# Normed head values by DMA crossbar instead of TensorE transposes, and r projected two heads later

## The reference, cut to what matters

```python
u = rms_norm(h, g_pre); proj = u @ w_in          # split: c_b c_c c_x c_z | q k v r lr_f lr_b | m_a m_b
y_conv = c_b * conv3(c_c * c_x) * silu(c_z);      p_conv = y_conv @ w_out_c
o = gla(q, k, v, g_f) + reversed_gla(q, k, v, g_b)   # 4 heads, 128 keys, 256 values each
o = rms_norm(o, gla_g)                            # per head and token, over its 256 values
y_gla = o * silu(r);                              p_gla = y_gla @ w_out_g
merged = sigmoid(m_a) * p_conv + sigmoid(m_b) * p_gla
out = h + rms_norm(merged @ w_out, g_post)
```

## Time and profile before

| | us |
|---|---|
| median of 3 runs (lowest, highest) | 2988.17 (2987.7, 2990.24) |
| profiled execution, its own time | 2986.59 |
| span of its slowest core, core 1 | 2985.0 |
| spans of the eight cores | 2977.7 to 2985.0 |
| granted TensorE clock, mean of each core | 0.995 to 0.997 |

### The profile page before, as it was taken

How to read it: one execution, slowest core, us unless ns; L and a number is a source line. 1 busy time by engine, 2 the same in 40 slices (tenths; PEclk the granted TensorE clock), 3 DMA queues, 4 the chain that set the end, 5 groups by cost and what they waited for, 6 DMA issues and landing times.

```text
span 2985.0 us, 54382 instructions; the slowest of 8 cores (2977.7 to 2985.0 us)
## 1 busy us (share of the span) xinstructions
PE 2923.8 (98%) x16828; PEld 1521.0 (51%) x16828; DVE 1575.0 (53%) x2467; ACT 1337.3 (45%) x2546; POOL 833.5 (28%) x1260
## 2 busy tenths in 40 slices
PE   6899999999999999999999999999999999999998
PEld 3465554444456655444455555444445655544443
DVE  4576771452567775153267677326227776723523
ACT  5666641231476663132167665223236666412211
POOL 3133243321322332142232223223122222311212
PEclk9899999999999999999999999999999999999999
DMA  7456557842632233273372223347245222323323
GB/s 183 80 101 132 98 146 156 233 135 78 172 92 63 54 85 98 75 231 105 92 188 61 55 63 80 103 126 210 78 128 145 57 64 57 107 75 106 118 77 124
DMA packets 258071, 330.56 MB, mean 111 GB/s; under 512 B 136432, under 2 KB 139376, under 8 KB 257280
## 3 DMA queue, kind: packets, MB, share of 16 engines
q1 hardware_dynamic: 244256, 301.73, 35.1%
q0 software_dynamic: 13536, 25.37, 5.9%
HBM read 265.80 MB, written 59.31 MB: 109 GB/s over the span
## 4 chain that ended last, share of the span: by engine, by line
PE 95%; DMA 1%; DVE 1%; issue 1%; ACT 1%; POOL 0%; SPq 0%; DVEq 0%; ACTq 0%; POOLq 0%
PE ps L477 94%; PE ps L482 1%; DMA sb_KT<-sb_GR 0%; DMA sb_onT<-x 0%; DVE sb_TF L507 0%; DMA sb_SM<-sb_GR 0%; ACT sb_GR L494 0%; ACT L494 0%; DMA sb_ycT<-x 0%; SPq L534 0%; DMA y<-sb_ycT 0%; DVE sb_ycT L503 0%; DVE sb_ycT L507 0%; POOL sb_stat L512 0%; ACT sb_AT L494 0%
## 5 line engine op out<-in xcount | busy, mean ns | idle before, releaser
L477 PE MATMUL ps<-sb_uT,sb_W 128*128 128x512 bf16 (+2 forms) x8960 | 1875.4, 367 | 4.0 <-ACT sb_onT L494 3.7
L477 PEld LDWEIGHTS ps<-sb_uT,sb_W 128*128 128x128 bf16 (+1 forms) x8960 | 818.7, 98 | 932.2 <-issue 19.5
L494 ACT ACTIVATE sb_CS<-ps 128x512 f32<-128x512 f32 (+2 forms) x640 | 348.6, 550 | 935.7 <-PE ps L477 933.5
L507 DVE SCALAR_TENSOR_TENSOR sb_CS<-sb_CS,ps 128x512 f32<-128x512 f32 x256 | 176.1, 688 | 686.2 <-PE ps L477 680.7
L503 POOL TENSOR_TENSOR sb_GR<-sb_CS 128x512 bf16<-128x512 f32 x128 | 162.2, 1268 | 692.9 <-DVE sb_CS L507 692.8
L477 PE MATMUL ps<-sb_GR 128*128 128x512 bf16 (+2 forms) x1792 | 348.7, 318 | 0.0
L507 DVE SCALAR_TENSOR_TENSOR sb_CS<-sb_CS,sb_convw 128x512 f32<-128x512 bf16 x256 | 215.1, 850 | 73.3 <-ACT sb_CS L494 58.6
L477 PE MATMUL ps<-sb_V,sb_uT 128*128 128x256 bf16 x2048 | 241.5, 273 | 0.0
L477 PEld LDWEIGHTS ps<-sb_GR 128*128 128x128 bf16 x1792 | 163.8, 98 | 135.6 <-issue 0.7
L477 PE MATMUL ps<-sb_onT,sb_W 128*128 128x512 bf16 x1024 | 231.5, 379 | 0.0
L503 POOL TENSOR_TENSOR sb_CS<-sb_CS 128x512 f32<-128x512 f32 x128 | 166.0, 1301 | 178.1 <-DVE sb_CS L507 160.8
(11 more groups left out here) (116 smaller groups left out, 2653.3 us busy)
## 6 DMA issues: line engine op xcount, KB each, us to landing
sb_W<-wsc SPq DMA_DIRECT2D x496, 256.0 KB, 2.8
sb_onT<-x SPq DMA_DIRECT2D x50, 512.0 KB, 5.7
sb_W<-w_all POOLq DMA_DIRECT2D x80, 256.0 KB, 5.3
sb_GR<-x SPq DMA_DIRECT2D x40, 512.0 KB, 5.3
wsc<-sb_W SPq DMA_DIRECT2D x80, 256.0 KB, 4.5
y<-sb_GR SPq DMA_DIRECT2D x32, 512.0 KB, 3.2
sb_ycT<-x SPq DMA_DIRECT2D x32, 512.0 KB, 5.1
y<-sb_ycT SPq DMA_DIRECT2D x32, 512.0 KB, 3.8
```

What stands on the lines that cost most here:

```text
L477: S.add("pe", lambda e: e.matmul(out, lhsT=lhsT, rhs=rhs, start=start, stop=stop), r, w, cost=max(0.025, free_n(rhs) / 2400.0 + 0.0025) / ...
L494: S.add("act", lambda e: e.activation(out=out, in_=in_, func=func, **kw), r, w, table=TABLE.get(func), cost=0.17 + 0.82e-3 * free_n(in_) + ...
L507: S.add("dve", lambda e: e.scalar_tensor_tensor(out=out, in0=in0, scalar=scalar, in1=in1, op0=op0, op1=op1), r, w, cost=0.21 + 1.05e-3 * f ...
```

## The change

The four TensorE transposes of a unit and their PSUM bank go away. A DMA transpose (`b_X`, on SP) takes the 128x512 values of ON straight to onT, which is now laid out by tile: for a head 16 tiles of 2 x 128 columns. ON has three buffers instead of two, and `b_O` of unit u asks for the transfer of unit u - 3 where it asked for the transposes of u - 2. r of head s - 2 is projected in step s, so r of head 2 in the last step of phase 1; that of head 3 follows behind it, and half of it stands inside `stage6`, ahead of the first og. Its Silu stays in its PSUM bank, which is held until `r_mul` on DVE multiplies it with `glag` and with onT, in place. og reads onT with a stride. The scan of `soft` is cut in two halves of 512, the loads of the next x into onT are contiguous, and the planner counts 3.5 us for a DMA transpose and has other values of `PWEIGHT` and `BACKLOG`.

```diff
+XBAR_LAT = 3.5
-PRESS, PWEIGHT = 4.0, 0.5
-BACKLOG = 4.0
+PRESS, PWEIGHT = 4.0, 1.0
+BACKLOG = 3.0
...
-        for c in ("M", "BO", "BS", "BT", "BM", "BN", "EM", ...
+        for c in ("M", "BO", "BS", "BX", "RM", "BM", "BN", "EM", ...
...
-        onT = [Buf("onT", j * 4096, 4096) for j in range(8)]
+        onT = [Buf("onT", h * 8192, 8192) for h in range(4)]
-        ON = [Buf("ON", i * KB, KB) for i in range(2)]
+        ON = [Buf("ON", i * KB, KB) for i in range(3)]
...
-            S.add("dve", lambda e: e.tensor_tensor_scan(out=r_ap, data0=smask[:], data1=r_ap, initial=0.0,
-                                                        op0=ALU.mult, op1=ALU.add), e_k + ["smask"], e_k, cost=2.3)
+            for z in range(2):
+                h_ap, h_k = e1(F32, d * 1024 + z * 512, 512)
+                r_ap = h_ap[:, ::-1] if d else h_ap
+                S.add("dve", lambda e, r_ap=r_ap: e.tensor_tensor_scan(out=r_ap, data0=smask[:], data1=r_ap, initial=0.0,
+                                                                       op0=ALU.mult, op1=ALU.add), h_k + ["smask"], h_k, cost=1.22)
...
-        def b_T2(H, u):
-            n0 = 6 - 2 * (u % 4)
-            tb, tbk = npsb()
-            for dvh in range(2):
-                for z in range(2):
-                    s_ap, s_k = ON[u % 2](BF16, z * 256 + dvh * 128, 128)
-                    c = dvh * 256 + (1 - z) * 128
-                    tr(tb[:, c:c + 128], s_ap, s_k, tbk)
-            for dvh in range(2):
-                o_ap, o_k = onT[H.hd * 2 + dvh](BF16, H.t0 + n0 * 128, 256)
-                stt(o_ap, tb[:, dvh * 256:(dvh + 1) * 256], glag[:, dvh:dvh + 1], o_ap, ALU.mult, ALU.mult,
-                    tbk + o_k + ["glag"], o_k)
+        def b_X(H, u):
+            n0 = 6 - 2 * (u % 4)
+            s_ap, s_k = ON[(H.hd * 8 + u) % 3](BF16)
+            o_ap, o_k = onT[H.hd](BF16, (H.half * 8 + n0) * 256, 512)
+            dtr(o_ap.rearrange("p (c k) -> p c k", c=4), s_ap, s_k, o_k, ("ox", (H.hd * 8 + u) % 3), 1 << 17)
+
+        def onv(j, t, n):
+            ap, keys = onT[j // 2](BF16, t * 256, n * 256)
+            keys = [k for i in range(n) for k in onT[j // 2](BF16, (t + i) * 256 + (j % 2) * 128, 128)[1]]
+            return ap.rearrange("p (i d k) -> p i d k", i=n, d=2)[:, :, j % 2, :], keys
...
-            bank, bk = nps()
+            bank, bk = nps(True)
             proj(h, 0, 128, s * 512, 512, bank, bk)
-            o_ap, o_k = onT[j](BF16, s * 512, 512)
-            act(o_ap, bank[:, 0:512], AF.Silu, bk, o_k)
-            if s == 3:
-                rel(h)
+            act(bank[:, 0:512], bank[:, 0:512], AF.Silu, bk, bk)
+            G["rb", j, s] = (bank, bk)
+
+        def r_mul(j, s):
+            bank, bk = G.pop(("rb", j, s))
+            o_ap, o_k = onv(j, 4 * s, 4)
+            stt(o_ap, bank[:, 0:512].rearrange("p (i k) -> p i k", i=4), glag[:, j % 2:j % 2 + 1], o_ap, ALU.mult, ALU.mult,
+                bk + o_k + ["glag"], o_k)
+            drop(bk)
...
+        def r_items(b, h, j, qs):
...
+            for q in qs:
+                put("RM", lambda q=q: r_mul(j, q), ("rm", b, j, q),
+                    [("r", b, j, q), ("X", b, j // 2, 7 - 2 * q), ("X", b, j // 2, 6 - 2 * q)])
+            return [(lambda q=q: unit(q), ("r", b, j, q), [("X", b, j // 2, 7 - 2 * q), ("X", b, j // 2, 6 - 2 * q)]) for q in qs]
...
+                    rj = 2 * (s - 2) + half if s >= 2 else None
+                    ca, cz, cbb, rh = conv_units(b, s // 4, 2 * (s % 4) + half, rj)
+                    ru = [] if rj is None else r_items(b, rh, rj, range(4))
+                    for (fn, name, aft) in ca + ru[0:2] + cz + ru[2:4] + cbb:
+                        put("D2", fn, name, list(aft) + ([("ST", b, 7)] if s < 4 else []))
+                    if s == 4 and half == 1:
+                        rr = [(w2.reserve(("r", j)), j) for j in (6, 7)]
+                        last = [[it for (h, j) in rr for it in r_items(b, h, j, qs)] for qs in ((3, 2), (1, 0))]
...
-                            pu = (b, s - 1, u - 2) if u >= 2 else (b, s - 2, u + 6)
+                            pu = (b, s - 1, u - 3) if u >= 3 else (b, s - 2, u + 5)
...
-                            put("BT", lambda H=H, u=u: b_T2(H, u), ("T2", b, s - 1, u),
-                                [("M", b, s - 1, u), ("r", b, 2 * s - 1, 3)])
+                            put("BX", lambda H=H, u=u: b_X(H, u), ("X", b, s - 1, u), [("M", b, s - 1, u)])
...
-            osrc = lambda c, s: onT[c](BF16, t0 + s * 512, 512)
+            osrc = lambda c, s: onv(c, hh * 8 + 4 * s, 4)
...
+                if n == "og" and d == 0:
+                    for it in late:
+                        put("D2", *it)
```

More of the change, by code:

```diff
@@ L87, in __init__, with add @@
         self.starts = None
-    def add(self, eng, fn, reads=(), writes=(), semkey=None, extra=(), cost=0.1, table=None, nbytes=0):
+    def add(self, eng, fn, reads=(), writes=(), semkey=None, extra=(), cost=0.1, table=None, nbytes=0, lat=DMA_LAT):
         op = Op(eng, fn, semkey)
@@ L129, in add @@
             self.free["dma"] = d0 + nbytes / DMA_RATE
-            op.end = self.free["dma"] + DMA_LAT
+            op.end = self.free["dma"] + lat
         else:
@@ L536, in dtr @@
         def dtr(out, in_, r, w, semkey, nbytes):
-            return S.add("sp", lambda e: e.dma_start_transpose(out, in_), r, w, semkey=semkey, nbytes=nbytes)
+            return S.add("sp", lambda e: e.dma_start_transpose(out, in_), r, w, semkey=semkey, nbytes=nbytes, lat=XBAR_LAT)
         def rot(name, bufs):
@@ L633, in program @@
         yout = [[Buf(r, o + i * 4096, 4096) for i in range(2)] for r, o in (("GR", 40 * KB), ("ycT", 8 * KB))]
-        xst = onT + [Buf("GR", i * 4096, 4096) for i in range(8)]
+        xst = [Buf("onT", i * 4096, 4096) for i in range(8)] + [Buf("GR", i * 4096, 4096) for i in range(8)]
         usX = [Buf("ycX", i * 2048, 2048) for i in range(2)]
@@ L1034, in ycT, with conv_units @@
             return Buf("ycT", j * 2048, 2048)
-        def conv_units(b, hh, j, r=False):
+        def conv_units(b, hh, j, r=None):
             t0 = hh * 1024
             pv = pvb[j % 2]
-            hs = {n: w2.reserve((n, j)) for n in (("cc", "cx", "r", "z", "cb") if r else ("cc", "cx", "z", "cb"))}
+            hs = {n: w2.reserve((n, j if n != "r" else r)) for n in (("cc", "cx", "z", "cb") if r is None else ("cc", "cx", "r", "z", "cb"))}
             me = (b, hh, j)
@@ L1244, in phase1 @@
                                 [("v",) + me + (3,)] + ([("qm",) + me + (1,)] if pr == 3 else []))
[L1247 to L1255, removed]
+                    rj = 2 * (s - 2) + half if s >= 2 else None
[6 more added lines that the diff above has]
+                        last = [[it for (h, j) in rr for it in r_items(b, h, j, qs)] for qs in ((3, 2), (1, 0))]
+                        for it in last[0]:
+                            put("D2", *it)
+                        late = last[1]
                     if s > 0:
@@ L1312, in stage6 @@
             ysrc = lambda c, s: ycT(hh, c)(BF16, s * 512, 512)
-            osrc = lambda c, s: onT[c](BF16, t0 + s * 512, 512)
-            for d in range(8):
-                hs = [p.reserve((n, d)) for p, n in ((w1, "ma"), (w2, "oc"), (w1, "mb"), (w2, "og"))]
-                for s in range(2):
-                    put("D2", lambda h=hs[0], d=d, s=s: gate(h, d, s, "ta"))
-                for s in range(2):
-                    put("D2", lambda h=hs[1], d=d, s=s: outp(h, d, s, "t1", ysrc), ("oc", b, hh, d, s))
-                for s in range(2):
-                    put("D2", lambda h=hs[2], d=d, s=s: gate(h, d, s, "tb"), ("mb", b, hh, d, s))
-                for s in range(2):
-                    put("D2", lambda h=hs[3], d=d, s=s: outp(h, d, s, "t2", osrc), ("og", b, hh, d, s),
-                        [("T2", b, 3, 7)])
+            osrc = lambda c, s: onv(c, hh * 8 + 4 * s, 4)
+            hs = {}
+            seq = [(n, d) for d in range(8) for n in ("ma", "oc", "mb", "og")]
+            if late:
+                seq.remove(("ma", 1))
+                seq.insert(3, ("ma", 1))
+            for (n, d) in seq:
+                hs[n, d] = (w1 if n[0] == "m" else w2).reserve((n, d))
+            for (n, d) in seq:
+                if n == "og" and d == 0:
+                    for it in late:
+                        put("D2", *it)
+                for s in range(2):
+                    if n[0] == "m":
+                        put("D2", lambda h=hs[n, d], d=d, s=s, n=n: gate(h, d, s, "t" + n[1]), (n, b, hh, d, s))
+                    else:
+                        put("D2", lambda h=hs[n, d], d=d, s=s, n=n: outp(h, d, s, "t1" if n == "oc" else "t2", ysrc if n == "oc" else osrc),
+                            (n, b, hh, d, s), [("rm", b, 7, 0)] if n == "og" else [])
         def cast_wo(d):
@@ L1390, in program @@
         for z in range(4):
[L1391 to L1393 removed]
+            ap, keys = onT[z](F32, 0, 1024)
+            xnext.append((ap, keys))
```

(8 more changed lines are left out.)

57 lines of the change are left out of this document (26 added, 31 removed).

## The result

The changed kernel is faster: the ratio of its runs to those of the kernel before is 0.9885, 95% interval 0.9865 to 0.9904. Executions in which one die ran over 1% longer than the other at a lower granted clock, or which were over 1.5% above the fastest, are left out of every ratio here. The profiled execution took 2953.35 us, and its slowest core was core 7.

The account below looks back on a forecast made before the run. TensorE, busy 98% of the span, was taken as the bound; - 28.4 + 4 + 1.6 + 3 = - 19.8 from 2986.6 gave 2966.8, forecast as 2968 for the median run; own range 2959 to 2979, 8 in 10 2951 to 2982.

Parts of the forecast that it names:

- rival 1: Sequence 0's key waits go, nothing added: 2951; or transposes cost up to their busy time: 2947; chance 0.10 for both.
- Transposes, - 28.4: Removing 512 TensorE transposes saves their distance to the next start: 128 groups of four at 0.222 us, 28.4 us.
- Sequence 0, + 3: Sequence 0's start: heads 0 and 1 lose r as filler while weights still arrive, costing 3 us.
- Rival 2: Sequence 0 starves without r in its first heads, losing 27.7 us: 2987.5, no change; chance 0.09.
- Phase 1, + 4: Phase 1: the longer chain of squares, norm and transfer makes TensorE wait 1 us per sequence, 4 us in all.
- The first og, + 1.6: Ahead of each sequence's first og, TensorE waits for the last r product: 0.4 us each, 1.6 us in all.
- Edits at nothing: Transfers on SP's queue, strided og reads, Silu in PSUM and halved scans were each taken to cost TensorE 0 us.
- Busy time "down by about 50 us": Sign in the profile after: TensorE's busy time falls by about 50 us where the span falls by 20.
- Rival 3: SP's queue: key transposes come late behind transfers waiting for DVE, TensorE stops; just slower up to 3038; chance 0.07.
- Rival 4: Phase 1: DVE or ACT takes over as the bound; chance 0.02 together with the rest.

Follow-up runs that it names:

- Run 1: Changed kernel with 512 dead TensorE transposes of the identity put back, four ahead of each r unit: 2981.0 us, ratio 0.9976.
- run 4: Kernel before, with only r of head 0 in sequence 0 moved behind the conv units of both halves of step 0: 2981.3 us, ratio 0.9977.
- run 3: Changed kernel with the old planner constants (PWEIGHT 0.5, BACKLOG 4.0): 2972.1 us, ratio 0.9946.
- run 7: Changed kernel with r projected one head later instead of two, behind the conv units, none left inside `stage6`: 2975.1 us, ratio 0.9956.
- run 2: Kernel before with only the new planner constants (PWEIGHT 1.0, BACKLOG 3.0, 3.5 us for a DMA transpose): 2977.4 us, ratio 0.9964.
- run 5: Changed kernel with two ON buffers and each of the 128 transfers issued a second time into an unread scratch buffer: 2975.6 us, ratio 0.9958.

## Why the prediction was right, and where its sum was off

Faster was right, and so was the main term; the size was 20 where 34 was measured. 2953.8 lies below the forecast's own range (2959 to 2979) and within the range of 8 in 10 because that took in rival 1, which had a chance of 0.10: in that much it was luck. By its own steps:

- **Transposes, - 28.4.** Right. Run 1 gives 27, and each period is 7.0 us shorter against 28.4 / 4 = 7.1. The 81 ns a matmul of the Trainium skill ("TensorE: Matmul & The Clock Gate", "Back-to-back issue gap") gives, by the estimate in the prediction, 41.5 us; run 1 does not agree, with 53 ns.
- **Sequence 0, + 3: the step that failed.** The prediction said that "heads 0 and 1 no longer have r to fill TensorE". Measured is 12.9 like for like less the 7.1 of the transposes: - 5.8 instead of + 3, 9 us of the 14 by which the sum was off. In step 0, r was not filler. It waited for the last input tile and held the conv units behind it; runs 4, 3 and 7 fill the window 75 to 125 us whenever r stands behind, with either set of constants. The prediction had named what happened, that the new order avoids the two key waits and wins 8.9 us, and did not take it. The row was in the prediction ("the first 150 us are the one stretch where TensorE waits"), and the second rival put it down to the input's norm and the key transposes, without asking which item stood first in D2.
- **Phase 1, + 4.** Measured: the three periods lose 21.0 where the transposes alone give 21.3, so + 0.3 where three sequences had + 3. The fear had ground: with the old constants it is 5 us a sequence (run 3). The prediction gave `PWEIGHT` and `BACKLOG` no price at all; run 3 puts them at 18 us in the new arrangement and run 2, with the 3.5 us for a DMA transpose, at 11 in the old.
- **The first og, + 1.6.** Measured 0.7, four waits of 0.2.
- **Edits at nothing** (transfers, stride, Silu in PSUM, scans): right together, since the periods leave 0.3 us for all of them; none was run alone, so a loss of one could hide behind a gain of another. The strided og reads take 379 ns as before; the scan in two halves costs 147.7 us of DVE against 144.8, beside TensorE's work.
- **Busy time "down by about 50 us"**: wrong, it is 26.3. The busy time of the engine counts a moment once, so the tails, under which the next matmul runs, were never in the difference. The group's 49.6 and the engine's total are two kinds of sum.
- **Rival 1** (2951) lies within 3 us of the result, and half for its own reason: both key waits went, 8.9 us, and one of 4.8 came elsewhere. **Rival 2** was the wrong way round. **Rival 3** stayed away in the kernel: TensorE has no wait for a `sb_SM` or `sb_CS` transfer; the one stop of run 5, 10.7 us, came by POOL's queue. **Rival 4**: DVE has 228 of 340 us and ACT 195, less than before.

What stays open: how the 5.8 us of sequence 0 divide between the place of r and the constants. Each alone gains more than that in the old kernel (7 and 11 us), so they are not additive: early arrival is given back, in runs 2 and 4 behind the first og (3.8 and 9.3 us), in the changed kernel between 150 and 450 us (7.5 us of the 13.6 won in the window before). In the changed kernel under the old constants nothing of it is left at the og of sequence 1 (run 3).

## What to carry to other kernels

Where one engine is 98% busy, the price of taking instructions off it is their distance to the next start times their count, and putting them back as dead work measures it. Before an item is called filler, look at what it waits for and what stands behind it in its chain: in an in-order chain an item that comes too early is a plug. Ask the same of every in-order queue: in run 5 one weight load ahead of a small instruction on POOL had its part in a stop of 10.7 us on TensorE. When a change moves the order that a planner makes, price the planner's constants as a part of the change: here they decided 18 of 34 us.

## What the runs showed of the hardware

- The changed kernel moves 347 MB instead of 331, and in more packets: the page after counts 322,327 DMA packets against 258,071, and 206,064 under 512 B against 136,432. The median landing of the 128 transfers is 2.8 us. At the end of sequence 0, with the DMA engines over 90% busy in most slices, the same transfer took 7.0 us in run 5 (median of four), and 8.5 in the changed kernel (of two). The key transposes that TensorE waited for landed as slowly: 11.7 us for the one at 121 us before, 9.8 for the one at 287 us after, where the medians are 3.1 and 3.3.
- A stop of TensorE costs more than its length. Behind the 4.78 us wait of the changed kernel the next eight matmuls of 128x512 start 0.43 us apart, and those behind them 0.22:

```profile
287.15 0.58 PE L478 MATMUL ps<-sb_GR,sb_KT 128*128 128x256 bf16 x2 [4.78 <-DMA sb_KT<-sb_GR]
287.53 3.62 PE L478 MATMUL ps<-sb_uT,sb_W 128*128 128x512 bf16 x8
290.95 0.59 PE L478 MATMUL ps<-sb_GR,sb_KT 128*128 128x256 bf16 x2
291.37 1.89 PE L478 MATMUL ps<-sb_uT,sb_W 128*128 128x512 bf16 x8
293.10 0.38 PE L478 MATMUL ps<-sb_GR,sb_KT 128*128 128x256 bf16 x2
```

```profile
287.00:291.00 4.00, 3.85 (x11) 1.51 (x12) 2.28 (x4) 1.79 (x2) 0.48 (x1) 0.50 0.17 61
```

The window's granted clock is 0.50, the lower of the two levels, 1.2 GHz. That stop cost 4.8 us and, in these eight matmuls, 8 x 0.21 = 1.7 us more.
